# Latent attention from the last block of queries to the first, beside stick-breaking rounds

## The reference

```
# stick-breaking, 8 heads of width 64, per block of 128 queries over the keys up to its end
z = q @ k.T / 8;  sp = softplus(z) where s < t, else 0
a = exp(log_sigmoid(z) - (reverse_cumsum(sp) - sp));  o_sb = a @ v
# latent attention, 4 heads, per block of 128 queries over the keys up to its end
s = (qn @ kn.T + qr @ kr.T) * MLA_SCALE;  s = -inf where key > query
o_mla = softmax(s) @ v
mixed = concat(rmsnorm(o_sb), rmsnorm(o_mla))
```

## Time and profile before

| what | value |
|---|---|
| median of 3 runs | 3455.55 us (3450.47 to 3455.75) |
| profiled execution | 3458.23 us, its span 3456.4 us |
| TensorE busy | 3206.3 us, 93% of the span |
| VectorE, ScalarE, GpSimd busy | 1443.4, 1097.4, 669.2 us |
| first latent step S0 starts | 409.28 us |
| scores of S19 start, the last round's values just behind | 600.49 us |
| S31's scores start, its values end | 717.46, 728.57 us |
| output projection phase begins | 743.33 us |

### The profile page before, as it was taken

One profiled execution on the slowest core, in us unless ns is written; L12 is line 12 of the kernel. 1 busy time (PEld: TensorE's weight loads), 2 busy tenths in 40 slices (PEclk: granted clock), 3 DMA queues, 4 the chain that ended last, 5 costly groups with the idle time before them and its releaser, 6 DMA issues. The chain is left out here.

```text
span 3456.4 us, 36380 instructions
## 1 busy us (share of the span) xinstructions
PE 3206.3 (93%) x14817; PEld 2466.1 (71%) x14817; DVE 1443.4 (42%) x1849; ACT 1097.4 (32%) x1632; POOL 669.2 (19%) x317
## 2 busy tenths in 40 slices
PE   6999988879999999995999999999999999999995
PEld 4765544447788888874767787777777888888874
DVE  3113333536414141475456877668552213223123
ACT  4334433323312030342453322223434323223122
POOL 2222111014222222242121000011111222222220
PEclk9999999889999999997999999999999999999997
DMA  3211000013111111123332121104334221221121
GB/s 125 97 63 60 19 0 1 1 64 108 49 49 46 48 48 49 49 89 137 100 108 92 37 68 44 61 34 141 110 110 164 92 98 49 98 98 49 49 92 55
DMA packets 105933, 246.19 MB, mean 71 GB/s; under 512 B 8232, under 2 KB 49448, under 8 KB 105640
## 3 DMA queue, kind: packets, MB, share of 16 engines
q1 hardware_dynamic: 97992, 215.56, 19.3%
q10 hardware_dynamic: 7776, 28.32, 2.0%
HBM read 187.74 MB, written 55.05 MB: 70 GB/s over the span
## 5 line engine op out<-in xcount | busy, mean ns | idle before, releaser
L1676 PE MATMUL psum<-normed_hi,w_hi 128*128 128x512 f32 x1632 | 674.3, 413 | 42.4 <-POOL w_lo L2218 35.2
L1678 PE MATMUL psum<-normed_hi,w_lo 128*128 128x512 f32 x1632 | 639.4, 392 | 0.0
L1677 PE MATMUL psum<-normed_lo,w_hi 128*128 128x512 f32 x1632 | 638.2, 391 | 0.0
L2218 POOL TENSOR_TENSOR w_lo<-buffer,w_hi 128x1024 fp32r<-128x1024 f32 x122 | 310.0, 2541 | 1500.8 <-ACT w_hi L1250 1500.8
L1676 PEld LDWEIGHTS psum<-normed_hi,w_hi 128*128 128x128 f32 x1632 | 308.8, 189 | 114.9 <-POOL w_lo L2218 36.7
L1678 PEld LDWEIGHTS psum<-normed_hi,w_lo 128*128 128x128 f32 x1632 | 307.6, 188 | 66.1
L1677 PEld LDWEIGHTS psum<-normed_lo,w_hi 128*128 128x128 f32 x1632 | 308.9, 189 | 63.7 <-issue 8.0
L2839 POOL TENSOR_TENSOR w_lo<-buffer,w_hi 128x1024 fp32r<-128x1024 f32 x88 | 212.4, 2415 | 724.9 <-ACT w_hi L2757 724.9
L1250 ACT ACTIVATE buffer<-psum,par 128x512 f32<-128x512 f32 (+1 forms) x196 | 138.0, 705 | 518.6 <-PE psum L1678 503.4
L2719 PE MATMUL psum<-hidden_hi,w_hi 128*128 128x512 f32 x512 | 200.9, 392 | 3.1 <-POOL w_lo L2839 3.1
L2719 PE MATMUL psum<-normed_hi,w_hi 128*128 128x512 f32 x512 | 200.1, 391 | 3.3 <-POOL normed_lo L2846 2.2
(11 more groups left out here) (393 smaller groups left out, 5438.5 us busy)
## 6 DMA issues: line engine op xcount, KB each, us to landing
buffer<-in_w_mlp SPq DMA_DIRECT2D x72, 512.0 KB, 3.6
buffer<-in_w_in SPq DMA_DIRECT2D x70, 512.0 KB, 4.9
scratch_in<-buffer ACTq DMA_DIRECT2D x54, 512.0 KB, 2.9
buffer<-in_w_gate SPq DMA_DIRECT2D x40, 512.0 KB, 3.6
buffer<-scratch_in SPq DMA_DIRECT2D x32, 512.0 KB, 6.5
buffer<-scratch_y SPq DMA_DIRECT2D x20, 512.0 KB, 7.7
buffer<-in_w_br SPq DMA_DIRECT2D x20, 512.0 KB, 3.6
buffer<-in_w_o SPq DMA_DIRECT2D x16, 512.0 KB, 3.7
```

Source lines behind the costliest of these rows:

```text
L1676: pe.matmul(out, hi, xh, start=k == 0, stop=False)
L1677: pe.matmul(out, hi, xl, start=False, stop=False)
L1678: mm = pe.matmul(out, lo, xh, start=False, stop=k == unit.kc - 1)
L2218: pool.tensor_tensor(ws.lo[:, n % 2], raw[:, n % 2], ws.hi[:, n % 2].bitcast(F32), ALU.subtract).then_inc(w_lo, 1)
```

## The change

The latent steps take the blocks of queries from 7 down to 0 instead of from 0 up to 7; the four heads of a block still follow one another. `rows_order` and `row_of(t)` replace `t // MLA_H` wherever a step's block is meant, also in the planned dates. `wide(t)` counts in the new order. A narrow step's wait for its own maximum now counts the halves of the wide steps ahead of it. The half of the latent output that is normalised amid the steps is the second half of the queries, since that is finished first.

```diff
+    rows_order = list(range(NB - 1, -1, -1))
+    def row_of(t):
+        return rows_order[t // MLA_H]
...
-        step_at.append(step_at[-1] + 5.6 + 4.4 * (min(t, T - 1) // MLA_H + 1) / NB)
+        step_at.append(step_at[-1] + 5.6 + 4.4 * (row_of(min(t, T - 1)) + 1) / NB)
...
-    OUT = [("sb", 0), ("sb", 1), ("mla", 0), ("mla", 1)]
+    OUT = [("sb", 0), ("sb", 1), ("mla", 1), ("mla", 0)]
     def wide(t):
-        return max(0, t + 1 - MLA_H * (HALF // P))
+        return sum(row_of(v) >= HALF // P for v in range(t + 1))
...
-                        b, h = t // MLA_H, t % MLA_H
+                        b, h = row_of(t), t % MLA_H
...
-                        for kb in range(w // MLA_H + 1):
+                        for kb in range(row_of(w) + 1):
                             mm = pe.matmul(l_ps[:, 0:P], vm[:, kb, w % MLA_H * P:(w % MLA_H + 1) * P], pt[:, kb * P:(kb + 1) * P],
-                                           start=(kb == 0), stop=(kb == w // MLA_H))
+                                           start=(kb == 0), stop=(kb == row_of(w)))
...
-                    n = (t // MLA_H + 1) * P
+                    n = (row_of(t) + 1) * P
...
-                            act.wait_ge(l_kept, T // 2 * (half + 1))
+                            act.wait_ge(l_kept, T // 2 * (n - 1))
...
-                            dve.wait_ge(max_done, t + 1)
+                            dve.wait_ge(max_done, t + 1 + wide(t))
...
-                        b = w // MLA_H
+                        b = row_of(w)
```

## The result

The changed kernel took 3487.95 us (median of 4 runs, 3486.08 to 3495.50), the kernel before, run beside it, 3453.01 (4 runs, 3450.39 to 3455.75): ratio 1.0102, 95% interval 1.0084 to 1.0120. It is slower, as forecast, by some 35 us where 15.5 were forecast, and lies 2 us above the range.

What follows compares the result with a forecast made beforehand. TensorE was read as 93% busy, with the latent steps' chains and clock setting a 319.3 us stretch. Terms 212.1 + 14 + 6.7 + 45.4 + 44.1 + 12 + 0.5 = 334.8, +15.5: 3471 us, range 3450 to 3486.

Steps and rivals of the forecast that it cites:

- The stretch: From the first latent step S0 to the end of the last step: 319.3 us before, 334.8 forecast, +15.5.
- The walk beside the rounds: S0 to S14 beside stick-breaking rounds, each period walked at full clock by planner dates: 212.1 us against 169 before.
- the tail: Time between the end of a round's sums and the next scores: 3.7 us before, 4.9 forecast for S7, S9 to S12.
- The exponential that I blamed: The step's exponential on ScalarE, put behind the round's by the dates in S7, S9 to S12: 1.1 us in the tail.
- 34 us of TensorE work: Plain part of the rise of 43 us beside the rounds: 15 long steps at 94.9 us, 19 short ones at 60.5.
- The clock beside the rounds: Falls to 1.2 GHz during S0 to S14: four of 6.8 us, costing 14 us; bounds 0 and 27 (eight falls).
- S15: First latent step running alone, behind the last round: 6.7 us.
- S16 to S20: Lone steps that take three output norms: 41.4 us walked plus 4 for slow clock, 45.4.
- S21 to the end: Lone steps of rows 2, 1 and 0: 44.1 us at full clock, 12 for slow clock, 0.5 for the last values.
- the bound of 15.7: Upper bound in us on the slow-clock cost of the lone steps of rows 2 to 0, if all run at 1.2 GHz.
- slower still: Rival: falls nearly every period beside the rounds (27 us), all lone steps slow; +32 us, 3487 us; chance 0.18.
- The rivals that ended faster or the same: Faster: clock stays at 2.4 GHz, -10.5 us, 3445, chance 0.12. Same: fewer falls, +0.5 us, 3456, chance 0.2.

Runs made afterwards that it cites:

- The added zeros: Changed kernel plus three matmuls of zeros behind the transposes of each step beside the rounds (S0 to S14): 3487.25 us, ratio 1.0094.
- the kernel with the exponential first: Changed kernel with the date share of the step's exponential on ScalarE moved from 0.3 to 0.2: 3475.15 us, ratio 1.0067 to the kernel before.
- The two kernels that part rows from dates: Turned rows with the dates of before: 3464.95 us, ratio 1.0037; rows of before with the dates of the change: 3475.25 us, ratio 1.0072.
- four fractions in the planner: Changed kernel with date shares moved: exponential 0.3 to 0.2, transposes 0.6 to 0.5, copies 0.8 to 0.6 and 0.55: 3445.06 us, ratio 0.9992.

## Why the prediction was right in direction and wrong in size

This goes through the prediction's own terms, against the profiled pair. The stretch came to 352.7 us, with 334.8 forecast: 17.9 too few.

- *The walk beside the rounds* (212.1): right. 235.8 less 27.3 for the clock is 208.4. S0 to S9, nearly all at full clock, took 148.2 with 144.1 walked. Within it, the last instruction of the tail was taken wrongly: "1.02 + 1.1 + 2.1 + 0.6 = 4.9" has ScalarE's copy last, and the VectorE copy behind L1107 made it 5.5 (the terms as written add up to 4.8). That looks small in time, but it is the wait that ended last, and the prediction has no term for VectorE in it. The exponential that I blamed is on the way to that copy, since it stands ahead of the Ln, but a date earlier by a tenth of a step took only 0.3 us off. The "34 us of TensorE work" do not follow from the prices named: by them the 15 long steps come to 85.4, 25 more than the short ones' 60.5. No term of the sum rests on them.
- ***The step that failed:* "The clock beside the rounds ... I take four falls of 6.8 us in all: 4 x 3.4 = 14."** Measured 54.5 us in six stretches, by half their length 27.3 us, the upper bound that I had named: 13.3 of the 17.9. I had counted that two of four like tails were followed by a fall, and applied the half to tails that were longer and held less. The four tails of S9 to S12, with waits of 2.8 us, each had one (552.2, 576.1, 593.1, 613.6), and three of them lasted 10 to 14 us, not 6.8; the tail of S13, with a wait of 1.93 us, had none. The added zeros show the clock as a cause: at full clock the same S10 to S13 are 17 us shorter. Whether the extra exponential as such brought the falls is not shown: with its date moved it stayed in the tail, and the falls made some 54 us as before. With the copies moved as well they made 27.
- *S15* 7.2 for 6.7, *S16 to S20* (to the scores of S21) 48.5 for 45.4: +0.5 and +3.1. The norms on short rows cost as walked, the slow clock a little more.
- *S21 to the end* 61.2 for 56.6 (44.1 + 12 + 0.5): +4.6. Every step was at 1.2 GHz, and the stretch lies 0.9 us beyond what the bound of 15.7 would give. A row-1 step took 5.6 us for the walked 4.1, a row-0 step 4.1 for 3.25.
- *Ends.* S0 starts 2.9 us earlier and the time behind the barrier is 2.5 shorter, which was not forecast and is no effect of the change that a run shows. So the profiled pair shows +27.9, and the medians +34.9; the 7 us between lie in which execution was profiled: that of before stood 5.2 above its median, that of after 1.9 below.

The rival "slower still" had the number (3487) and most of the mechanism, and the chance 0.18. All lone steps were slow. But its 27 us beside the rounds were meant as a fall nearly every period, and came as six falls in 15 periods, longer ones: there the number is in part luck. The range stopped at 3486, inside it. The rivals that ended faster or the same needed the clock to stay up; it did so only once the order or the added matmuls helped.

The rule of the Trainium skill ("TensorE: Matmul & The Clock Gate", section "HAM oscillation — how this bites in real kernels") has short waits harmless. It gave the faster result and is not borne out: falls followed waits of 2.84 us with little matmul work around them, the lone steps, with waits of some 0.4 us, stayed at 1.2 GHz, and in the kernel with the exponential first the clock fell at 705.6 and 719.2 with no wait above 0.65 us in the steps ahead.

The forecast took the dates only as what decides who stands where. The two kernels that part rows from dates show that the dates are two thirds of the loss. The walk has both in it, so this does not contradict it, but the long rows beside the rounds are the smaller part.

## What to carry to other kernels

When a plan moves long work beside short, list for each in-order engine what stands ahead of the instruction that frees the next buffer, on every engine that writes a part of it: the last of them sets the wait. Then ask whether what is to be moved can start any earlier: an instruction that is ready only when its neighbour is stays in the chain wherever it stands. Do not price the clock by a share of falls seen behind other tails: here a period that repeated with the same long tail had its fall four times out of four. And before giving up a reordering, try its dates: here four fractions in the planner were worth more (38 us) than the change itself had cost.

## What the runs showed of the hardware

**The same steps at either clock.** The changed kernel and the one with the exponential first do the same work from S20 on, at different clocks. Timeline of the changed kernel, scores of S25:

```profile
724.42 1.22 PE L761 MATMUL psum<-k_low,buffer 128*128 128x256 f32 x2 [0.47 <-ACT buffer L964]
```

and of the kernel with the exponential first, scores of S25 and S27:

```profile
713.65 0.70 PE L761 MATMUL psum<-k_low,buffer 128*128 128x256 f32 x2 [0.47 <-ACT buffer L964]
...
721.82 1.22 PE L761 MATMUL psum<-k_high,buffer 128*128 128x256 f32 x2 [0.47 <-ACT buffer L964]
```

The wait ahead is the same 0.47 us, and the pair of S25 takes 1.22 in the one and 0.70 in the other. In the second kernel the clock rose at 688.4, ahead of the scores of S20, stood at 1.2 GHz from 705.6 to 709.0 and fell again at 719.2, in S26, with no wait above 0.65 us in the steps ahead. What decides the rise was not found; it is worth up to 13 us to a kernel, and no step of the walk could have told it.

**Zeros that pay.** Three matmuls of zeros behind the transposes (2.15 us at 384 wide) made S10 to S13 17 us shorter, where TensorE otherwise waits 2.8 us, and the same three cost 8.6 over S0 to S4, where its waits ahead of the scores are at most 1.6. They did not keep every fall away: with them in S9 to S13 alone, S10 still stood at 0.73.
